# The token mixer of a two-layer decoder trunk: block transposes on VectorE, half-width inverse levels, stacked sequence updates, 16 gate columns, column squares, and a written-out order

## The reference, cut to what matters

```python
tmat = bb[..., :, None] * kk * d_strict + jnp.eye(chunk, dtype=jnp.float32)
u = lax.linalg.triangular_solve(tmat, bb[..., None] * vb, left_side=True, lower=True)
...
def step(s, inp):
    qd, kt, uc, wc, qkc, el = inp
    nv = uc - jnp.einsum('bhlk,bhkv->bhlv', wc, s)
    o = jnp.einsum('bhlk,bhkv->bhlv', qd, s) + jnp.einsum('bhij,bhjv->bhiv', qkc, nv)
    s = el[..., None, None] * s + jnp.einsum('bhlk,bhlv->bhkv', kt, nv)
    return s, o
```

## Time and profile before

| | |
|---|---|
| median of three runs | 1502.56 us (1497.63 to 1502.75) |
| the profiled execution | 1502.63 us, its span 1500.8 us |
| TensorE busy | 1456.8 us |
| VectorE busy | 866.9 us |
| ScalarE busy | 620.3 us |
| mean granted TensorE clock | 0.983 |

### The profile page before, as it was taken

The page is one execution under the profiler, slowest core; times in us unless marked ns, Lnnn a source line. Parts: engine busy times, 40 slices in busy tenths (PEclk is TensorE's granted clock), DMA queues, the critical chain, the costliest instruction groups (busy, mean ns, idle before and its releaser), DMA issues.

```text
span 1500.8 us, 22849 instructions
## 1 busy us (share of the span) xinstructions
PE 1456.8 (97%) x9628; PEld 1417.3 (94%) x9628; DVE 866.9 (58%) x1448; ACT 620.3 (41%) x980; POOL 36.3 (2%) x124
## 2 busy tenths in 40 slices
PE   9999998999999999999999999999999999999997
PEld 8999998889989999999999999998799899999997
DVE  5655434876367665553376554347763776655433
ACT  5443333553324453333354433346532244544432
POOL 0000001010000000000000000010100000000000
PEclk9999999999999999999999999999999999999999
DMA  6544344221114334434435443442211143444342
GB/s 244 200 141 141 125 141 156 85 85 61 58 57 157 109 138 149 142 130 135 159 127 197 141 141 125 151 145 85 85 62 57 57 177 108 146 146 163 125 151 97
DMA packets 49461, 191.24 MB, mean 127 GB/s; under 512 B 6000, under 2 KB 8432, under 8 KB 48848
## 3 DMA queue, kind: packets, MB, share of 16 engines
q1 hardware_dynamic: 48752, 184.66, 35.9%
q0 software_dynamic: 608, 5.12, 0.8%
HBM read 183.33 MB, written 6.43 MB: 126 GB/s over the span
## 4 chain that ended last, share of the span: by engine, by line
PE 90%; DVE 5%; ACT 3%; issue 1%; DMA 1%; SPq 0%; ACTq 0%; DVEq 0%
PE PS L1402 25%; PE PS L1404 24%; PE PS L1403 24%; PE PS L1561 5%; PE PS L1442 2%; PE PS L1443 2%; PE PS L1447 2%; DVE WL L997 2%; PE PS L1559 1%; PE PS L1727 1%; DVE CV L1127 1%; ACT WH L728 1%; PE PS L1679 1%; PE PS L1596 0%; DMA RAW<-in_w_in 0%
## 5 line engine op out<-in xcount | busy, mean ns | idle before, releaser
L1402 PE MATMUL PS<-XH,WH 128*128 128x336 f32 (+1 forms) x1728 | 555.1, 321 | 6.3 <-DVE WL L997 6.3
L1404 PE MATMUL PS<-XH,WL 128*128 128x336 f32 (+1 forms) x1728 | 544.7, 315 | 0.0
L1403 PE MATMUL PS<-XL,WH 128*128 128x336 f32 (+1 forms) x1728 | 544.5, 315 | 0.0
L997 DVE TENSOR_TENSOR WL<-RAW,WH 128x1024 fp32r<-128x1024 f32 (+1 forms) x312 | 398.5, 1301 | 195.5 <-ACT WH L728 195.5
L728 ACT ACTIVATE WH<-RAW 128x1024 fp32r<-128x1024 f32 (+1 forms) x312 | 343.1, 1118 | 201.8 <-DMA RAW<-in_w_down 171.5
L1402 PEld LDWEIGHTS PS<-XH,WH 128*128 128x128 f32 x1728 | 326.0, 189 | 27.2 <-issue 24.3
L1403 PEld LDWEIGHTS PS<-XL,WH 128*128 128x128 f32 x1728 | 326.3, 189 | 0.0
L1404 PEld LDWEIGHTS PS<-XH,WL 128*128 128x128 f32 x1728 | 326.0, 189 | 0.0
L1402 PE MATMUL PS<-HH,WH 128*128 128x336 f32 (+1 forms) x704 | 221.0, 314 | 0.0
L1404 PE MATMUL PS<-HH,WL 128*128 128x336 f32 (+1 forms) x704 | 220.4, 313 | 0.0
L1403 PE MATMUL PS<-HL,WH 128*128 128x336 f32 (+1 forms) x704 | 220.2, 313 | 0.0
(11 more groups left out here) (232 smaller groups left out, 1331.3 us busy)
## 6 DMA issues: line engine op xcount, KB each, us to landing
RAW<-in_w_up SPq DMA_DIRECT2D x176, 512.0 KB, 4.2
RAW<-in_w_down SPq DMA_DIRECT2D x64, 704.0 KB, 4.1
RAW<-in_w_in SPq DMA_DIRECT2D x56, 512.0 KB, 4.2
RAW<-in_w_out SPq DMA_DIRECT2D x16, 512.0 KB, 4.7
SEQ_S<-in_states SPq DMA_DIRECT2D x2, 2048.0 KB, 10.2
out_state_s<-SEQ_S POOLq DMA_DIRECT2D x2, 2048.0 KB, 7.7
X<-in_x SPq DMA_DIRECT2D x8, 168.0 KB, 4.1
out_y<-X SPq DMA_DIRECT2D x4, 320.0 KB, 2.3
```

The costliest lines, as they stand in the source:

```text
L997: dve.tensor_tensor(WL[slot][:, cols], RAW[slot][:, cols], WH[slot][:, cols].bitcast(F32), ALU.subtract).then_inc(split_lo.sem, 1)
L1402: pe.matmul(out, wh, xh, start=first, stop=False)
L1403: pe.matmul(out, wh, xl, start=False, stop=False)
L1404: return pe.matmul(out, wl, xh, start=False, stop=last)
```

## The change

1. `nt` and `mirror` leave TensorE and ScalarE: VectorE transposes MI into NI, and NI into MI, in 32x32 blocks (below level 32 the matrices are block-diagonal in them); at level 32 it transposes only the four corner blocks of each head row.
2. `x` below the last level computes only the even blocks' columns, 64 per head, and `y` takes 64 columns; the mask multiplication is over 128x256.
3. `sn` contracts over 128 partitions in fp32r: KSP and VSP hold high and low parts of 32 tokens' keys and values in four groups of 32 partitions, so that one matmul of 512 columns adds the products. `key_hi`, `key_twin`, `val_hi`, `val_twin` on ScalarE and `key_lo`, `val_lo` on VectorE build them.
4. `gate_rows` has 16 weight columns, high parts beside low parts: two matmuls a block in place of three.
5. `sq_sum` sums the squares straight into columns with three one-column products; `sq_rows` and `sq_cols` go.
6. `gb` and `rob` are transposes of a broadcast column.
7. The order is a table; `read` is eight half steps.
8. At the boundaries TensorE runs `keep_busy` products before and behind the rows. The load into the slot of the last chunk but one of an FFN begins when its first 1024 columns have been used.

The core of the diff:

```diff
+HEAD = [
+    ("entry",), ("gate_rows",), ("evac", 0), ("evac", 1), ("gate_read",), ("tap", 0), ("tap", 1), ("hi", 1, 0), ("evac", 2),
+    ("hi", 1, 1), ("conv", 0), ("gate_cols",), ("lo", 1, 0), ("silu", 0), ("conv", 1),
+]
...
+    [("evac", 11), ("x", 2, 2)],
+    [("read", 0), ("read", 1), ("conv", 10), ("evac", 12), ("y", 2, 2), ("lo", 5, 0)],
...
+    [("val_lo", 1), ("evac", 21), ("spread", 1, 0), ("tap", 21), ("key_lo", 1), ("x", 1, 64), ("o", 0), ("spread", 2, 0),
+     ("key_twin", 1), ("rob", 2), ("conv", 19), ("lo", 10, 1), ("st", 0), ("sn", 1, 0), ("o_low", 2), ("yt", 1, 64), ("hi", 11, 0)],
+    [("sn", 2, 0)],
+    [("kt", 1), ("spread", 3, 0), ("val_twin", 1), ("conv", 21), ("ks", 1), ("spread", 0, 1)],
...
+    steps = list(HEAD)
+    for now, work in enumerate(BEHIND_PART):
+        steps.append(("part", FIRST_TILE + now // PARTS, now % PARTS))
+        steps += work
+    return steps
...
+                    if old[1] in LAST_BUT_ONE:
+                        sp.wait_ge(first_cols.sem, first_cols.at(LAST_BUT_ONE.index(old[1]), old[0]))
+                        load_half(layer, c, 0)
...
+                    elif what == "val_hi":
+
+                        act.wait_ge(evac["dve"].sem, evac["dve"].at(LEFT_PSUM["nv", C_TILE][1], layer))
+                        for q in VAL_HI[t]:
+                            ins = act.activation(VSP[t][quad(q), :, :], NVP[quad(t), C_TILE, :, :], ACT.Copy)
+                        ins.then_inc(val_hi.sem, 1)
...
+                    elif what == "nt":
+                        dve.wait_ge(pair_set.sem, pair_set.at(NTH["unit", t], layer))
+                        dve.transpose(flat(NI[:, t, :, :]), flat(MI[:, t, :, :])).then_inc(turned.sem, 1)
+                    elif what == "mirror":
+
+                        _, t, m = step
+                        own(("y", t, m), layer)
+                        if m < SQUARE:
+                            ins = dve.transpose(flat(MI[:, t, :, :]), flat(NI[:, t, :, :]))
+                        else:
+                            for low in range(0, P, 2 * SQUARE):
+                                top, bottom = slice(low, low + SQUARE), slice(low + SQUARE, low + 2 * SQUARE)
+                                ins = dve.transpose(MI[top, t, :, bottom], NI[bottom, t, :, top])
+                        ins.then_inc(mirrored.sem, 1)
...
+                            low = blocks(mask(name), m, 0).unsqueeze(1).to_broadcast([P, HEADS, P // (2 * m), m])
+                            evacuated(dve.tensor_tensor(by_blocks(XB[t][:, :, 0:P // 2], m), half_bank(step, m), low, ALU.mult))
...
-                        dve.tensor_tensor(buf[0:N_SAMPLE, :, :], per_seq, which, ALU.mult).then_inc(seq_spread.sem, 1)
+                        dve.tensor_tensor(buf[:, :, :], per_seq, which, ALU.mult).then_inc(seq_spread.sem, 1)
...
+            def keep_busy(n):
+
+                for _ in range(n):
+                    pe.matmul(PS[:, 6, 0:P], mask("ident"), mask("ident"), start=True, stop=True)
...
+                last = (layer, j) == (DEPTH - 1, 2)
+                if not last:
+                    keep_busy(2 if j == 1 else 4)
                 pe.wait_ge(y_inv.sem, y_inv.at(j, layer))
                 rows(RC[:, 1, :], Y_ROWS).then_inc(y_rows.sem, 1)
+                if not last:
+                    keep_busy(7)
...
+                        for q in range(TT):
+                            ins = pe.matmul(QK_COLS[:, q, t:t + 1], SQX[t % 2][:, tcols(q)], mask("ones", 1), start=True, stop=True)
+                        ins.then_inc(sq_summed.sem, 1)
...
+                            if kt == KT - 1:
+                                pe.matmul(GATE_ROWS[0:2 * HEADS], W8X[:, kt, 0:2 * HEADS], xl, start=False, stop=False)
+                                ins = pe.matmul(GATE_ROWS, W8X[:, kt, :], xh, start=False, stop=True)
...
-                        per_head_products(step, layer, lambda h: G[:, t, h:h + 1].to_broadcast([P, P]),
-                                          lambda h: incl(t))
+                        pe.wait_ge(to_act.sem, to_act.at(1, layer))
+                        per_head_products(step, layer, lambda h: GC[:, t, h:h + 1].to_broadcast([P, P]), None, transpose=True)
...
+                            for h in range(HEADS):
+                                ins = pe.matmul(half_bank(step, m)[:, h, :, :], DA[:, t, h, :], blocks(NI[:, t, h, :], m, 0),
+                                                start=True, stop=True)
...
+                        for h in range(HEADS):
+                            ins = pe.matmul(heads_bank(step)[:, h, 0:P // 2], MI[:, t, h, :], XB[t][:, h, 0:P // 2],
+                                            start=True, stop=True)
...
+                        pe.matmul(heads_bank(step), KSP[half][:, h, :], SEQ_BUF[NTH[step] % 2][:, :, :],
                                   start=True, stop=True).then_inc(filled.sem, 1)
```

More of the change, by code:

```diff
@@ L60 @@
 LAST_CHUNK = (AT_IN - 1, AT_UP[1] - 1, CHUNKS - 1)
+LAST_BUT_ONE = (LAST_CHUNK[0] - 1, LAST_CHUNK[2] - 1)
 SLOTS = 3
@@ L81 @@
 PART_KT = [(0, 3), (3, 6), (6, KT)]
[L82 to L86, removed]
+SQUARE = 32
+QUAD = 32
+READS = 2 * HEADS
 TILES = [("qkv", n) for n in range(6)] + [("z", 0), ("qkv", 6), ("qkv", 7), ("z", 1), ("qkv", 8), ("z", 2), ("qkv", 9), ("z", 3),
@@ L111, in chunk_length @@
     return D_LEN if any(at <= c < at + N_DOWN for at in AT_DOWN) else A_LEN
[L114 to L155, removed]
@@ L452, in decoder_trunk @@
         dd_raw, dd_exp = sig("dd_raw", TT), sig("dd_exp", TT)
-        pair_set = sig("pair_set", TT)
+        pair_set, turned = sig("pair_set", TT), sig("turned", TT)
+        mirrored = sig("mirrored", sum(len(levels) - 1 for levels in LEVELS.values()))
         filled = sig("filled", len(GROUP_ORDER))
@@ L908, in mixer @@
                         evacuated(act.activation(QKM[:, t, :, :], heads_bank(step), ACT.Exp))
-                    elif what == "nt":
-                        evacuated(act.activation(NI[:, t, :, :], group(step, layer), ACT.Copy))
-                    elif what == "mirror":
-                        evacuated(act.activation(MI[:, step[1], :, :], group(step, layer), ACT.Copy))
                     elif what == "vt":
@@ L1277, in mixer @@
                         even = blocks(NI[:, t, :, :], m, 0)
-                        evacuated(dve.tensor_tensor(even, even, blocks(group(step, layer), m, 0), ALU.subtract))
+                        group(step, layer)
+                        evacuated(dve.tensor_tensor(even, even, half_bank(step, m), ALU.subtract))
                     elif what == "yt":
@@ L1304, in mixer @@
                         evacuated(ins)
+                    elif what == "key_lo":
+                        dve.wait_ge(key_hi.sem, key_hi.at(NTH["key_hi", t], layer))
+                        dve.tensor_tensor(KSP[t][quad(KEY_LO[t][0]), :, :], KTL[quad(t), C_TILE, :, :],
+                                          KSP[t][quad(t), :, :].bitcast(F32), ALU.subtract).then_inc(key_lo.sem, 1)
+                    elif what == "val_lo":
+                        dve.wait_ge(val_hi.sem, val_hi.at(NTH["val_hi", t], layer))
+                        dve.tensor_tensor(VSP[t][quad(VAL_LO[t][0]), :, :], NVP[quad(t), C_TILE, :, :],
+                                          VSP[t][quad(t), :, :].bitcast(F32), ALU.subtract).then_inc(val_lo.sem, 1)
                     elif what == "spread":
@@ L1569, in mixer, with mirror_made @@
             def mixer(layer):
+                def mirror_made(t, m):
+                    pe.wait_ge(mirrored.sem, mirrored.at(NTH["mirror", t, m], layer))
                 if layer == 0:
-                    pe.wait_ge(in_masks, 32)
+                    pe.wait_ge(in_masks, 48)
                 for step in STEPS:
@@ L1663, in mixer @@
                         t = step[1]
-                        evacuated(("mirror", t, step[2] // 2), layer)
+                        mirror_made(t, step[2] // 2)
                         per_head_products(step, layer, lambda h: XB[t][:, h, :], lambda h: MI[:, t, h, :])
@@ L1675, in mixer @@
                             pe.wait_ge(q_decayed.sem, q_decayed.at(ORDER.index(C_TILE), layer))
-                        for s in range(SEQS):
+                        for s in range(half * SEQS // 2, (half + 1) * SEQS // 2):
                             own = slice(s * SEQ_T, (s + 1) * SEQ_T)
```

326 lines of the change are left out of this document (168 added, 158 removed), and 7 rows, old and new, of the table BEHIND_PART.

## The result

The changed kernel takes 1439.34 us (median of 4 runs, 1438.96 to 1441.22) against 1501.62 for the kernel before, measured beside it (1497.63 to 1502.75): ratio 0.9592, 95% interval 0.9572 to 0.9613. It is faster by 62 us, 10 more than forecast. The forecast of 1450.6 lies 11 us too high, the range of 1438 to 1468 holds the time. The profiled execution took 1441.22 us, span 1439.4.

A forecast was written before the change was run, and what follows sets the result against it. TensorE, busy 97% of the span, was taken as the bound. Work off it 37.3 us, waits 2.4, clock 4.0, boundaries 7.1 and early load 1.2 sum to 52.0: 1502.6 - 52.0 = 1450.6 us, range 1438 to 1468.

The forecast's parts named there:

- (a): Mixers: nt and mirror groups leave TensorE, 30 groups at 0.44 us, 13.2 us less for both layers.
- (b): Mixers: gb and rob turn from products into transposes on TensorE, 12 groups, 5.4 us less.
- (c): Mixers: sn becomes one split-format pass on TensorE, 16 x 0.87 = 13.9 us less, bounds 11 to 15.
- (d): gate_rows: 16 instead of 24 matmuls of 336 columns on TensorE, 2.4 us less.
- (e): Mixers: half-width x and y groups save TensorE almost nothing, 0.02 us a group, 1.0 us for 48 groups.
- (f): Column squares: three one-column products at 0.64 us instead of 0.66, small transposes gone, 1.4 us less for both layers.
- VectorE: Mixers: net 7.6 us more VectorE work per layer, full transposes at 0.6 us each, VectorE 81% busy.
- Waits in the mixer: TensorE's waits in each mixer fall from 7.2 to 6 us a layer, 2.4 us gained for both.
- rival 3: Waits fall to 2 us a layer and boundaries return 10 us instead of 7.1: 1440 us, chance 0.15.
- Clock in the mixer: Lower-clock windows behind a 2.15 us wait and, by a quarter, behind the read go: 4.0 us gained.
- Boundaries and early load: keep_busy raises the clock at five boundaries, 7.1 us; an earlier weight load ends the SQY wait, 1.2 us net.
- Rival 5: The new table orders the mixers badly and waits take back all but a few us: about 1500 us, chance 0.03.

The follow-up runs named there:

- e5: The changed kernel's operations put in an order made by the planner of the kernel before: 1502.06 us.
- e7: The changed kernel with nt and mirror transposes back on TensorE, evacuated by ScalarE: 1465.37 us.
- e8: The changed kernel with sn as before (64 rows, fp32, 512 columns) and no steps for the stacks: 1452.75 us.
- e6: The kernel before with its own operations in the order of the new table: 1496.81 us.
- e4: The changed kernel with x and y at full width again (128 columns): 1440.83 us.
- e10: The changed kernel with all eight half steps of read side by side where the last one stood: 1452.5 us.
- e2: The kernel before with only the keep_busy products of the change added: 1495.51 us.
- e12: The changed kernel with spread(3, 0) done nine times over on VectorE, to make TensorE wait once a mixer: 1452.13 us.
- e9: e5 with the changed kernel's opening, both hi(1) steps ahead of gate_cols and the third eviction: 1502.32 us.
- e3: The changed kernel with each full VectorE transpose done twice in a row: 1445.72 us.

## Why the prediction was right, and where it was off

**Sign, bound and place: right.** TensorE was the bound, what left it was gained in full in this order (not in e5's), and the mixers give nearly all. Of the forecast 52.0 us, 43.7 were in the mixers, which gave 59.8. The busy time of 162 us that was to show it is a chance match: it was forecast for the shorter stretch of the earlier trace rows, and the 162.24 measured belong to the longer one, which had 186.58.

**(a) Transposes.** 6.6 us of work a layer forecast, 7.4 and 8.9 in e7's two mixers. Right in kind, undersized by 0.8 a layer or more: 0.49 a group where it was priced at 0.44.

**(b) gb and rob: undersized.** Priced as 0.89 less 0.44, 0.45 a group. The 48 instructions of gb and rob before span 6.15 us a layer in the trace, 1.03 a group, all at a clock of 1.00; after, 24 take 2.40, 0.40 a group. That is 0.63, 1.1 us a layer more. Why these groups took 1.03 where others take 0.89 is not shown.

**(c) sn: right.** 13.9 forecast; 13.4 by e8's median, 15 by its mixers alone.

**(d) gate_rows: the work went, about half of the gain did not come.** Of the 1.2 us of eight matmuls a layer, 0.55 are paid back by the wait for RC. The prediction took "all on the path" for granted and did not ask what TensorE would now reach too early. The 0.99 for ACCX is mainly the price of the table's opening, which the prediction didn't ask about either: e5, with the short gate_rows and the old opening, has no such wait (281.01 above); e6, with the long gate_rows and the new opening, has 0.6 a mixer.

**(e), (f): right.** 1.6 in e4 for a forecast 1.0. A sum of squares takes 0.60, forecast 0.64. By the Trainium skill, page "TensorE: Matmul & The Clock Gate", section "Back-to-back issue gap", the isolated gap would give a 64-column group half the time of a 128-column one; the section itself says that at small column counts this gap is too short for a stream of weight loads and matmuls, and the rows (0.87 against 0.89) and e4 bear that out.

**VectorE: right in the sum.** +7.3 us for a forecast +7.6, and that is partly luck: a full transpose takes 0.70, not 0.6, a mirror at level 32 0.6 instead of 0.4 (two pieces of 0.3). That is 1.7 more together, and what made up for it is not shown. The estimate of 1.24 worked out from the Trainium skill's page "VectorE: DVE Perf Modes", section "The three transpose paths", is too high.

**Waits in the mixer: the step that failed.** The mixers gave 16.1 us more than forecast: 8.8 of it is here, 7.3 is busy time ((a), (b), (c) and the clock, each by a little). Forecast 6 a layer, measured 1.6: 4.4 a layer, 8.8 us in all. Nearly half of it, 4 us, is an error in the working. The 2 us at sn(2, 0) counted 2.0 us of VectorE for the step conv(19), as for "an h tile". Tile 19 is a b tile; it has no convolution, and the step is empty. Without it VectorE is done in time, as it was (st(0) ended at 411.46, sn(2, 0) began at 411.61). The rest was caution: apart from sn(2, 0), the prediction kept most of the 7.2 because "others come", with no place named. In before's first mixer the waits were 2.1 us for the weights, 1.8 for SQX, 1.1 for MI, 1.1 ahead of sn and 0.9 in two small ones; none of them is left in after, whose 1.6 are the two new ones. That is rival 3, which gave 1440 us: its waits came about, its 10 us at the boundaries did not.

**Clock in the mixer: right in kind, half the size.** Forecast 4.0 for both layers. The mean goes from 0.98 to 1.00, 0.02 x 194 = 3.9 us a layer by that rounded mean and 3.3 by the prediction's own two windows (1.7 + 1.6): some 7 for both. The read was given only a quarter since reads 0 and 1 still stand side by side. In after these two bring nothing down; all eight do (e10), and so do e5's pairs with one part between them in its first mixer, though not in its second, where the clock is 1.00 at the reads.

**Boundaries and early load: oversized.** 7.1 + 1.2 forecast, 5.7 measured together, 4 to 6 of it keep_busy's. The early load was not tried by itself, and its 1.2 is not shown: in the kernels with it no wait for SQY is left, but without it that wait is 1.5 us in before, 0.9 in e6 and 0.2 in e2.

**Rival 5 (bad order): not what came, but the alternative it named is real.** e5 is that case with a price: the same operations in the planner's order stand at 1502, no faster than before. The prediction gave the table 2.4 us of waits and 4 us of clock. e5 and e6 show what it is worth: in the two mixers together the order alone gains 4 us, the operations alone lose 4 to 6, both together gain 60. It is an interaction. As we read it, the old plan spaces its steps for TensorE's longer work, so with shorter work TensorE reaches some operands early, waits, and runs on at the lower clock; the new table without the new operations waits for MI. The waits are in the traces; that the plan's spacing causes them is argued, not tried.

What stays open: how e5's first wait comes to be followed by 28 us of low clock, where e12's longer one is followed by 4 to 6 us. In e5 other waits and short matmuls (sums of squares, gates) follow it; e9 moved the waits instead of removing them, so the share of each isn't known. Nor is it known why the clock fell at the reads in e5's first mixer and not in its second.

## What to carry to other kernels

Work that left the engine that is the bound was gained here only when the order was made anew (e5 against after): ask at each operand whether the engine now arrives too early, and check the granted clock of the stretch, not just the list of waits. The one wait of 4.3 us tried here cost one and a half times its length, and 64 narrow matmuls in a row cost 5 to 7 us that the same ones spread among wide ones did not. When you replay an order by hand, look up what each step really issues; one empty step, counted as 2 us a layer, was the largest error here that has a name.

## What was not expected of the hardware

The granted clock fell to 0.50 while TensorE was busy without a gap, in a row of 16-column matmuls (e10, 371.63 to 381.95; the clock fell at about 375), and the mixers' busy time grew by 6.6 and 5.1 us. In after, a wait of 0.99 us is followed by a clock of 1.00; one of 2.15 in before by 7 us at a mean of 0.76 (291.78 to 298.78), and one of 4.27 in e12 by 0.50 until 423. A 512-element block transpose of 4-byte elements on VectorE costs 704 ns, as much as a tensor_tensor of that size (682), and one of 32 x 128 303 ns. Nearly nine us of added VectorE work a layer cost 3 us (e3), although VectorE was already busy 84% of the mixer.
